# The last 256 columns of a decoder step in two parts by tokens, and its final norm by token tile

## What is computed

```
def _rms(x, g):
    xf = x.astype(jnp.float32)
    y = xf * lax.rsqrt(jnp.mean(xf * xf, axis=-1, keepdims=True) + EPS)
    return (y * g.astype(jnp.float32)).astype(x.dtype)
...
    y = (jax.nn.silu(gc) * u) @ W['w_ffn_out'][l]
...
        x = x + f
...
    return _rms(x, W['norm_final']), stacked
```

## Time and profile before

| | us |
|---|---|
| median of 3 runs | 2161.26 (2159.86 to 2165.28) |
| the profiled execution | 2164.31 |
| its span, first to last instruction | 2162.6 |
| PE busy | 2072.0 (96%) |
| DVE busy | 1226.2 (57%) |
| ACT busy | 709.7 (33%) |
| POOL busy | 274.1 (13%) |

### The profile page before, as it was taken

How to read it: one execution, slowest core, us unless ns; L and a number is a source line. 1 busy time by engine, 2 the same in 40 slices (tenths; PEclk the granted TensorE clock), 3 DMA queues, 4 the chain that set the end, 5 groups by cost and what they waited for, 6 DMA issues and landing times.

```text
span 2162.6 us, 37265 instructions
## 1 busy us (share of the span) xinstructions
PE 2072.0 (96%) x15230; PEld 1870.5 (86%) x15230; DVE 1226.2 (57%) x2033; ACT 709.7 (33%) x1087; POOL 274.1 (13%) x241
## 2 busy tenths in 40 slices
PE   8999899999999999999998999899999999999997
PEld 6756797889979999999996577669988999999996
DVE  4467377765354666336635899664444566526652
ACT  5344334433242222112234325442332322212222
POOL 0022003532000000000003235320000100000000
PEclk9999999999999999999999999999999999999998
DMA  6478224324462232232224125642443222223221
GB/s 206 134 238 294 91 78 127 119 72 138 155 225 64 78 88 79 79 88 79 76 79 133 50 78 197 197 128 88 156 166 131 79 79 87 80 79 88 79 74 53
DMA packets 221612, 249.26 MB, mean 115 GB/s; under 512 B 18578, under 2 KB 175644, under 8 KB 221238
## 3 DMA queue, kind: packets, MB, share of 16 engines
q1 hardware_dynamic: 199322, 196.35, 28.5%
q0 software_dynamic: 9872, 28.65, 4.2%
q10 hardware_dynamic: 12248, 21.88, 3.1%
HBM read 233.63 MB, written 13.00 MB: 114 GB/s over the span
## 4 chain that ended last, share of the span: by engine, by line
PE 86%; DVE 7%; ACT 2%; issue 2%; PEld 1%; DMA 0%; POOL 0%; ACTq 0%; PEldq 0%; DVEq 0%
PE PS L862 56%; PE PS L840 11%; PE PS L924 5%; DVE stat L2615 1%; PE PS L1308 1%; PE PS L1502 1%; PE PS L1326 1%; PE PS L1615 1%; PE PS L1634 1%; PE PS L1337 1%; DVE arena L2522 1%; PE PS L1687 1%; PE PS L1002 1%; PE PS L1175 1%; PE PS L1349 1%
## 5 line engine op out<-in xcount | busy, mean ns | idle before, releaser
L862 PE MATMUL PS<-xr_r,WH 128*128 128x288 f32 (+2 forms) x1920 | 570.3, 297 | 0.8 <-POOL W_r L695 0.8
L862 PE MATMUL PS<-hT_r,WH 128*128 128x288 f32 (+2 forms) x1856 | 551.6, 297 | 4.2 <-issue 2.2
L862 PE MATMUL PS<-hT_r,W_r 128*128 128x288 f32 (+2 forms) x1856 | 550.5, 297 | 0.0
L2470 DVE TENSOR_TENSOR W_r<-W,WH 128x1024 fp32r<-128x1024 f32 (+1 forms) x219 | 282.1, 1310 | 339.6 <-ACT WH L1776 338.9
L862 PE MATMUL PS<-arena_r,WH 128*128 128x224 f32 (+2 forms) x1920 | 437.7, 297 | 1.5 <-issue 1.5
L1776 ACT ACTIVATE WH<-W 128x1024 fp32r<-128x1024 f32 (+1 forms) x262 | 266.5, 1034 | 453.0 <-PE PS L862 286.8
L862 PEld LDWEIGHTS PS<-xr_r,WH 128*128 128x128 f32 x1920 | 363.1, 189 | 1.5 <-issue 1.5
L862 PEld LDWEIGHTS PS<-hT_r,WH 128*128 128x128 f32 x1856 | 350.7, 189 | 6.5 <-issue 6.5
L862 PEld LDWEIGHTS PS<-hT_r,W_r 128*128 128x128 f32 x1856 | 350.6, 189 | 0.0
L862 PEld LDWEIGHTS PS<-arena_r,WH 128*128 128x128 f32 x1920 | 324.6, 189 | 2.7 <-issue 2.5
L862 PE MATMUL PS<-arena_r,W_r 128*128 128x288 f32 (+2 forms) x704 | 208.7, 296 | 0.0
(11 more groups left out here) (443 smaller groups left out, 3028.7 us busy)
## 6 DMA issues: line engine op xcount, KB each, us to landing
W<-in_w_ffn_in SPq DMA_DIRECT2D x176, 256.0 KB, 3.3
W<-in_w_ffn_out SPq DMA_DIRECT2D x40, 512.0 KB, 3.4
W<-in_w_in_ab SPq DMA_DIRECT2D x28, 512.0 KB, 3.7
C<-in_cache_mem_k SPq DMA_DIRECT2D x10, 1024.0 KB, 8.9
C<-in_cache_diff_k POOLq DMA_DIRECT2D x32, 256.0 KB, 4.8
C<-in_cache_diff_k SPq DMA_DIRECT2D x32, 256.0 KB, 4.2
W<-in_w_xk SPq DMA_DIRECT2D x16, 512.0 KB, 3.6
W<-in_w_xv SPq DMA_DIRECT2D x16, 512.0 KB, 3.8
```

What stands on the lines that cost most here:

```text
L862: ins = mm(o, w[:, k, c * 128:c * 128 + 128], v(k0 + k)[:, t0:t1], start=opens and first and k == 0 and e == 0, stop=last and k == nk - 1 ...
L2470: v_.tensor_tensor(slot_view(WL, NW, n), slot_view(W, NW, n), plain(slot_view(WH, NV, n)), ALU.subtract).then_inc(lo_done, 1)
```

## The change

The last block of `down11` is taken out of the common loop (`last_block`). Its pieces are cut by tokens: first both chunks for tokens 0 to 255 through all three slots, then both chunks for the other 320 through all three slots again. The first part has one bank, the second two. DVE adds the parts apart.

The final norm no longer uses `yT`, the squares on ACT in turned form, POOL's additions and the products with ones. PE turns `xT` itself: the first four chunks of the five tiles between the slots of the first part, the other four of tiles 0 and 1 after the first slot of the second part, those of tiles 2 to 4 at the end, with three banks instead of two. ACT squares each turned tile out of PSUM and sums by token in the same instruction (`turned_squares`). The weight of the final norm lies as a row on all partitions (`gain_row`, one load of 512 KB on SP's queue behind the first slot of `down10`). DVE multiplies the first half of each tile by it (`first_halves`), later takes the reciprocal, scales the second half out of PSUM by root and weight in one instruction, and scales the first half in place (`finish_tile`). The root is made tile by tile by ACT (`tile_root`). SP stores each tile as soon as it is scaled and waits for the stores at its end.

```diff
+        EARLY = 256
+        LAST_PIECES = ((0, 0, EARLY, 0, True), (1, 0, EARLY, EARLY, False), (0, EARLY, TOK, 512, True), (1, EARLY, TOK, 1024, True))
...
+                    if n == first_slot["down10"]:
+                        sp.dma_start(L["gain_row"], A["norm_final"].unsqueeze(0).to_broadcast([128, D])).then_inc(gain_in, 16)
...
+            for i, (c0, rows) in enumerate(COLS):
+                sp.wait_ge(y_scaled, i + 1)
+                y = O["y_p"][c0:c0 + rows, :] if i < 4 else O["y_s"].rearrange("b t d -> (b t) d")
+                sp.dma_start(y, L["y"][i][0:rows]).then_inc(y_out, 16)
+            sp.wait_ge(y_out, 16 * NTILE)
...
-            for name in ("xo1", "down11"):
-                add_squares(name)
+            add_squares("xo1")
...
-                    if at == 3 and l == DEPTH - 1:
-                        turn_back(0)
...
+                                     blocks=ORDER[name][:-1] if name == "down11" else None)
+                if l == DEPTH - 1:
+                    conv_rows(3)
+                    last_block()
+
+            def turn_back(half, tiles):
+                for i in tiles:
+                    c0, rows = COLS[i]
+                    tr_unit("D", [(c * 128, xT[:, 4 * half + c, c0:c0 + rows]) for c in range(4)])
+
+            def last_block():
+
+                pj.align(3)
+                xh, xl = aX
+                before = pj.count("D", len(pj.who))
+                u = [open_bank("D") for _ in range(3)][0]
+                slots = []
+
+                def sums(piece, slot, first, closes, owed=False):
+                    c, t0, t1, off, opens = LAST_PIECES[piece]
+                    wh, wl, k0, nk, _, _ = slots[slot]
+                    for k in range(nk):
+                        for e, (v, w) in enumerate(((xh, wh), (xh, wl), (xl, wh))):
+                            ins = mm(fset(u)[:, off:off + t1 - t0], w[:, k, c * 128:c * 128 + 128], v(k0 + k)[:, t0:t1],
+                                     start=opens and first and k == 0 and e == 0, stop=closes and k == nk - 1 and e == 2, skip_group_check=True)
+                            if owed and k == 0 and e == 0:
+                                ins.then_inc(w_free, 1)
+                    return ins
+
+                turned = ((0, 1), (2, 3), (4,))
+                for n, slot in enumerate(slots_of(ORDER["down11"][-1])):
+                    slots.append(slot)
+                    for piece in (0, 1):
+                        ins = sums(piece, n, n == 0, slot[5], owed=n == 0 and piece == 0)
+                    if slot[5]:
+                        ins.then_inc(y_first, 1)
+                    if n == 0:
+                        pe.wait_ge(proj_dve, before)
+                    turn_back(0, turned[n])
+                for n, slot in enumerate(slots):
+                    for piece in (2, 3):
+                        ins = sums(piece, n, n == 0, slot[5])
+                    if slot[5]:
+                        ins.then_inc(proj_done, 3)
+                    if n == 0:
+                        pe.wait_ge(y_early, 1)
+                        turn_back(1, (0, 1))
+                tj.use(5 if u % NBANK == 0 else 2, 6, 7)
+                pe.wait_ge(proj_dve, pj.count("D", len(pj.who)))
+                turn_back(1, (2, 3, 4))
...
-            turn_back(1)
-            mean_by_token("down11")
...
                     if b == 2 and l == DEPTH - 1:
-                        turn_back(0)
+                        ahead(len(stream))
+                        for i in range(NTILE):
+                            turned_squares(0, i).then_inc(y_squares, 1)
+                            act.wait_ge(y_squares, i + 1)
...
+            def turned_squares(half, i):
+                rows = COLS[i][1]
+                n = tj.add("D")
+                act.wait_ge(tr_done, n + 1)
+                return fn(L["y_sq"][0:rows], tbank(tj.at[n])[0:rows, :], ACT.Square,
+                          accum_out=(sd if half else ss)[0:rows, i:i + 1])
+
+            def tile_root(i):
+                rows = COLS[i][1]
+                step(turned_squares(1, i))
+                if i == 0:
+                    act.wait_ge(y_bias, 1)
+                fn(hsd[0:rows, i:i + 1], sd[0:rows, i:i + 1], ACT.Sqrt, bias=ms[0:rows, i:i + 1], scale=1.0 / D).then_inc(y_root, 1)
...
-            roots_by_token()
-            act.wait_ge(hrs_ready, 3)
-            for i in (1, 3):
-                step(fn(L["y"][i], L["y"][i], ACT.Copy, scale=hrs[:, i:i + 1]))
-                store(O["y_p"][i * 128:i * 128 + 128, :], L["y"][i])
-            for n, i in enumerate((0, 2)):
-                act.wait_ge(y_scaled, n + 1)
-                store(O["y_p"][i * 128:i * 128 + 128, :], L["y"][i])
-            act.wait_ge(y_scaled, 3)
-            store(O["y_s"].rearrange("b t d -> (b t) d"), L["y"][4][0:64])
+            for i in range(NTILE):
+                if i == 2:
+                    tj.use(5 if (len(pj.who) - 3) % NBANK == 0 else 2, 6, 7)
+                tile_root(i)
...
-                            else:
-                                dve.wait_ge(proj_dve, pj.count("D", len(pj.who)))
-                                v_.tensor_scalar(L["yT"][:, c, :], xT[:, c, :], gain, None, ALU.mult).then_inc(y_half, 1)
...
+            def first_halves():
+                dve.wait_ge(gain_in, 16)
                 for i, (c0, rows) in enumerate(COLS):
-                    tr_copy("A" if i % 2 else "D", L["y"][i][0:rows, 512 * half:512 * half + 512], view=lambda t: t[0:rows, :])
+                    t = tr("D")
+                    dve.wait_ge(y_squares, i + 1)
+                    v_.tensor_tensor(L["y"][i][0:rows, 0:512], t[0:rows, :], L["gain_row"][0:rows, 0:512], ALU.mult).then_inc(tr_dve, 1)
+                v_.tensor_scalar(ms, ss, 1.0 / D, EPS, ALU.mult, ALU.add).then_inc(y_bias, 1)
+
+            def finish_tile(i):
+                rows = COLS[i][1]
+                t, y, r = tr("D"), L["y"][i][0:rows], hrs[0:rows, i:i + 1]
+                dve.wait_ge(y_root, i + 1)
+                step(v_.reciprocal(r, hsd[0:rows, i:i + 1]))
+                v_.scalar_tensor_tensor(out=y[:, 512:D], in0=t[0:rows, :], scalar=r, in1=L["gain_row"][0:rows, 512:D],
+                                        op0=ALU.mult, op1=ALU.mult).then_inc(tr_dve, 1)
+                v_.tensor_scalar(y[:, 0:512], y[:, 0:512], r, None, ALU.mult).then_inc(y_scaled, 1)
+
+            def last_block():
+                u = [pj.add("D") for _ in range(3)][0]
+                both = xT[:, KC - 2:KC, :]
+                early, late = (fset(u)[:, a:z].rearrange("p (c t) -> p c t", c=2) for a, z in ((0, 512), (512, 1536)))
+                dve.wait_ge(y_first, 1)
+                v_.tensor_tensor(both[:, :, 0:EARLY], both[:, :, 0:EARLY], early, ALU.add).then_inc(y_early, 1)
+                for i in range(2):
+                    finish_tile(i)
+                tj.use(5 if u % NBANK == 0 else 2, 6, 7)
+                dve.wait_ge(proj_done, pj.uses(u + 3))
+                v_.tensor_tensor(both[:, :, EARLY:TOK], both[:, :, EARLY:TOK], late[:, :, 0:TOK - EARLY], ALU.add).then_inc(proj_dve, 3)
+                for i in range(2, NTILE):
+                    finish_tile(i)
...
-            rstd_by_token()
-            dve.wait_ge(hrs_ready, 3)
-            dve.wait_ge(tr_dve, tj.count("D", len(tj.who)))
-            for i in (0, 2, 4):
-                rows = COLS[i][1]
-                y = L["y"][i][0:rows]
-                v_.tensor_scalar(y, y, hrs[0:rows, i:i + 1], None, ALU.mult).then_inc(y_scaled, 1)
```

44 lines of the change are left out of this document (19 added, 25 removed).

## The result

| | before | after |
|---|---|---|
| median us (6 executions each, taken together) | 2161.14 | 2150.26 |
| range us | 2159.86 to 2167.57 | 2145.76 to 2154.56 |
| the profiled execution, its span | 2164.31, 2162.6 | 2151.74, 2150.0 |

The ratio is 0.994 (95% interval 0.9928 to 0.9953), so the kernel is faster by 0.6%, a small gain but clear of the spread. The medians lie 10.9 us apart. The forecast was 2147.0 with a range of 2142 to 2154, so the median is 3.3 us above it and inside the range. In a second set of executions (5 after, 9 before) the ratio is 0.9948 (0.9932 to 0.9965).

A forecast was written before the change was run, and what follows sets the result against it. PE, with 86% of the last chain, bounds the kernel, so gains come only where it stands or has finished. Gains 3.7 + 10.7 = 14.4 us off 2161.26 give 2146.9, called 2147; own range 2143.5 to 2150.5, with rivals 2142 to 2154.

The forecast's parts named there:

- both places: PE's 6.9 us before the last 120 matmuls and the 20.1 us after the last matmul; gains 3.7 and 10.7 us.
- The mis-sized term: Kernel's end: the last store of 256 KB takes 2.7 us to the end of the span; bound above 5.1.
- The stands of PE: Convolution turns to last matmul: no stand over 0.3 us; 16.2 us of matmuls plus 3.2 of turns.
- Both thin margins: Last block: banks free before PE's turns, at 2124.5 for tile 2 (wanted 2126.2), 2128.3 for tile 4 (2128.7).
- The rival of stalled turns: Last block: every turn waits for ACT and DVE, 6.9 us stay, 2150.6 us; chance 0.08.
- the old 6.9 us: Kernel before, from the end of the convolution turns to the last 120 matmuls; 2.5 us of it a stand.
- Tiles 0 and 1: Their second half, in the last block: done at about 2138.2, 0.6 us before DVE's late addition, table load off the path.
- The tail: Last matmul to the end of the span: 9.4 us instead of 20.1, gain 10.7.
- The rival of tiles without overlap: Tail: tiles pass ACT and DVE without overlap (+2.2), last store costs 5.1 us (+2.4); 2151.5 us; chance 0.12.
- the forecast that each store runs alone: Tail: two stores before the last matmul and three after, each alone; 512 KB takes 1.3 us, so none piles up.
- The load of the same size at 2.6 us: A 256 KB load on SP's queue, 2.6 us from issue to landing, taken to confirm the last store's 2.7 us.
- The rival of 2166.8: Last block: clock falls to 0.5 and stays, 19.4 us of PE's work become 38.8; chance 0.04.

The follow-up runs named there:

- e1: Changed kernel with all 20 first-half turns ahead of the last block again, in two banks: 3.70 us more to the last matmul; ratio 0.9952.
- e2: Changed kernel with no store before all five tiles are scaled: 8.17 us from the last DVE instruction to the end instead of 3.35.
- e3b: Changed kernel without the cut by tokens, all five tiles finished after the block, small tile's first-half turn in the second slot: +3.67 us in all.
- e4: Changed kernel with the weight row loaded four times, each waited for: last stretch 29.89 us, where the changed kernel has 29.82.
- e5: Changed kernel with the small tile finished third and the root's table loaded early: +0.4 us in all; ratio 0.9938.
- e7: Changed kernel with the last store in two halves on two queues: 3.05 us from the last DVE instruction to the end instead of 3.35.
- g1: Changed kernel run once more, unaltered, five executions: last stretch 29.87 us, span 2144.9 instead of 2150.0; ratio 0.9948.
- g2: Same edit to the changed kernel as e7, five executions: 3.09 us from the last DVE instruction to the end; ratio 0.9945.
- e6: Changed kernel cut at 384 tokens instead of 256, with early table load and three banks for the second-half turns: +0.24 us in all.

## Why the prediction was right

The mechanism was right in both places, and the time came out inside the range. It wasn't exact: in the profiles the gain is 14.2 us against a forecast of 14.4, the medians differ by 10.9. One term was mis-sized, and in another two errors cancel.

**The stands of PE.** Forecast: none over 0.3 us from the convolution turns to the last matmul. Measured: none. From the end of those turns to the last matmul it was to be 19.4 us and was 19.0 (2140.03 - 2121.00). 120 matmuls took 16.0 (16.2), 28 turns 3.06, that is 0.109 each (0.115). Both thin margins held; ACT passes a tile in 0.72 us where the forecast had 0.78:

```profile
2124.34 0.60 ACT L2319 ACTIVATE arena<-PS 128x512 f32<-128x512 f32 x1 [1.29 <-PE PS L933]
...
2125.06 0.60 ACT L2319 ACTIVATE arena<-PS 128x512 f32<-128x512 f32 x1
```

e1 showed that the place of the turns earns this term. The rival of stalled turns would have been 3.7 us, and e1, which makes that rival real, measured 3.70. That the two agree to the last digit is luck, since the rival's 3.7 was the old 6.9 us with its addition, square and slow clock in it.

**Tiles 0 and 1.** They were to be done 0.6 us before DVE is wanted, and were done 0.7 us before. ACT after, in order of time:

```profile
2135.11 1.28 ACT L2327 ACT_TABLE_LOAD   x1
2136.41 0.29 ACT L2327 ACTIVATE misc<-stat 128x1 f32<-128x1 f32 x1
2136.61 0.58 ACT L2319 ACTIVATE arena<-PS 128x512 f32<-128x512 f32 x1
```

The root starts 0.02 us after the load's end. The Trainium skill ("ScalarE: Activation LUTs", "What ACT_TABLE_LOAD costs") puts a drain of about 1.38 us behind it. No such time is to be seen here; if part of it lies elsewhere, no row shows it.

**The tail.** From the last matmul to the last scaled tile: forecast 6.7, measured 6.62, but two errors cancel in it. Four turns and the root took 0.67 and 0.30 (0.46 and 0.24): the first turn behind a wait isn't pipelined with one before. DVE's pace was 1.25 us a tile (1.37), and ACT's 0.90 (1.1), so DVE is the bound as forecast. That the sum fits to 0.1 us is therefore partly luck. The rival of tiles without overlap fell with this.

**The mis-sized term.** The last store was taken at 2.7 us and took 3.35. I had 0.8 to its first bytes, 1.0 for the bytes and 0.9 behind them. In the rates after, the bytes fill four slices of 0.325 us and a little more at 200 GB/s, 1.3 us. They start 1.1 us after DVE's last instruction, right behind those of the large store ahead, and 0.95 us follow them. So the forecast that each store runs alone was also not quite true: the two before the last run without a gap, 1.3 us each at DVE's pace of 1.25. The rates of before had shown the small store's own: the fall to 290, 265, 214 and 164 at their end was it, and I read these four slices as 1.0 us. The load of the same size at 2.6 us, which seemed to confirm the term, was no measure of this store.

**The sum.** In the profiles the last stretch is 14.2 us shorter (43.99 - 29.82), forecast 14.4: 4.0 in the block (3.7) and 10.2 in the tail (10.7). e1, e2 and e3b account for 3.7, 4.8 and 3.7 of it one at a time (1.28 of e3b's is the table load). The other 2.0 weren't taken apart: the products for the mean (20 in 3.75 us at a clock of 0.50), the weight multiplies and the wide scalings are gone, and terms that overlap don't add up.

**The clock.** The rival of 2166.8 is refuted: the clock is 1.00 from the convolution turns to the last matmul, with turns between the streams, and the same stretch takes 19.83 to 19.85 us in all seven profiles that leave it as it is (after, e2, e4, e5, e7, g1, g2). The Trainium skill's account of gaps between groups of matmuls ("TensorE: Matmul & The Clock Gate", "HAM oscillation — how this bites in real kernels") doesn't reach this case, as the turns leave PE no gap. In e1 three stands of 0.5 to 1.3 us didn't bring the clock down either, but that is one profile, and in other stretches of this kernel the clock falls in some executions and not in others.

**What stays open.** The two sets of executions taken together have means of 2149.7 (11 after) and 2162.3 (15 before), 12.5 us apart with a standard error of 1.2 (from spreads of 3.0 and 2.9). The profiles say 14.2. If each execution's time less 1.7 and less its kernel's last stretch is taken as the start of that stretch, 35 executions of the changed kernel and its variants start it at 2118.0 on average and 31 of the kernel before at 2117.0, with a standard error of 0.6 for the difference. So a delay of up to some 2 us that the change causes earlier can't be excluded; the later first instructions in g1's comparison would fit one, and no single place for it was found. The other part that is uncertain is the 43.99 itself. It comes from the only profile of the kernel before, and there the clock was down in the turns and in the mean's products. Whether it is down there in every execution isn't known, and where it isn't, the last stretch of before is shorter and the gain smaller.

## What to carry to other kernels

At the end of a kernel, cut the last block so that part of the output is complete while the matrix engine still works on the rest. Let each finished tile leave at once. Here the cut was worth 3.7 us (1.28 of it a table load that an earlier root can hide as well) and the early stores 4.8, of 14. Put small dependent pieces of PE's work between long streams, so that the engines that empty their banks have a stream's time to do it (3.7 us). Price the last transfer by the rate of a transfer of its own shape (here 200 GB/s and not 400). When a stream is cut, price each part by the measured step for its length: at 192 columns the step was still that of 224, and three tiles early instead of two lost on PE what it won in the tail. When a load is delayed, count only the delay beyond what its queue would have waited anyway.

## What the runs showed of the hardware

- A matmul of 192 columns steps at 0.111 us (e6), like one of 224; 256 at 0.120 (2.88/24) and 320 at 0.147 (3.52/24) in the changed kernel, 384 at 0.174 (e6).
- A store of 64 partitions (256 KB) moves at about 200 GB/s, one of 128 partitions (512 KB) at about 400 (after, e5). With the small one halved on two queues the kernel ends 0.3 us earlier (e7, g2).
- Executions of one kernel differ by up to 9 us here, while the last 30 us of the changed kernel repeat to 0.05. Between its two profiles 1.5 us of difference are there at 24 us and 5.7 at 260 us, and what comes in between goes with stretches of 10 us whose mean granted clock is 0.83 to 0.86 in one and 1.00 in the other.
- The granted clock stayed at 1.00 behind three stands of 0.55, 1.33 and 0.94 us (e1), and was 0.54 in the turns of before behind a stand of 2.5 us, each in one profile.
- The load of the root's table takes 1.28 us, and the root starts 0.02 us behind it (after).
